# Hybrid decoder layer on one core: repairs at five seams, and transposes ahead of scores in the prompt's attention

## The reference

```python
def decoder_layer(x, nsa_fn, ...):
    xn = rmsnorm(x, g_mix)
    q, kvc, kvs, kvw, gt, mu, mv, mo, mi, mf = split(xn @ w_in)
    o_cmp, o_sel, o_win, ... = nsa_fn(q, kvc, kvs, kvw)
    gates = sigmoid(gt)
    o_nsa = gates[0] * o_cmp + gates[1] * o_sel + gates[2] * o_win
    o_nsa = rmsnorm(o_nsa, g_nsa)
    o_m, ... = mlstm_mixer(mu, mv, mo, mi, mf, ...)   # 4 heads of 128
    h = x + concat([o_m, o_nsa]) @ w_out
    up, f_new = causal_dwconv(rmsnorm(h, g_ffn) @ w_up, f_buf, w_fconv)
    a, g = split(up, 2)
    y = h + (silu(g) * a) @ w_down

def mlstm_mixer(...):
    uc = silu(causal_dwconv(u, conv_buf, w_conv) + b_conv)
    q, k = uc @ w_q, uc @ w_k                          # per head
    hs, C, n, m = mlstm_chunk_scan(q, k, v, ig, fg, C0, n0, m0)
    return (rmsnorm(hs, g_head) + skip * uc) * sigmoid(o)
```

## Time and profile before

| what | us |
|---|---|
| median of 3 runs | 1076.31 |
| lowest, highest | 1075.5, 1076.8 |
| the profiled execution, its own time | 1076.65 |
| its span from first to last instruction | 1074.9 |
| TensorE busy | 1018.1 (95%) |
| VectorE busy | 612.9 (57%) |
| ScalarE busy | 404.1 (38%) |
| GpSimd busy | 152.7 (14%) |

### The profile page before, as it was taken

The page is one execution under the profiler, slowest core; times in us unless marked ns, Lnnn a source line. Parts: engine busy times, 40 slices in busy tenths (PEclk is TensorE's granted clock), DMA queues, the critical chain, the costliest instruction groups (busy, mean ns, idle before and its releaser), DMA issues.

```text
span 1074.9 us, 19288 instructions
## 1 busy us (share of the span) xinstructions
PE 1018.1 (95%) x7776; PEld 917.0 (85%) x7776; DVE 612.9 (57%) x1305; ACT 404.1 (38%) x759; POOL 152.7 (14%) x207
## 2 busy tenths in 40 slices
PE   4999998999999979989899999999999999999996
PEld 4999998999866647665559999999999999999996
DVE  3736753444267656677957336676767677932222
ACT  4223422333143346448764333333333333621212
POOL 3200020330112221016740000000000000000000
PEclk9999999999999989999999999999999999999999
DMA  6561162553511165334012222222222222332322
GB/s 185 186 180 40 56 205 79 209 184 138 240 44 42 42 259 198 122 110 141 2 59 100 78 81 82 81 81 81 81 81 81 81 81 56 91 93 65 96 54 88
DMA packets 82074, 114.26 MB, mean 106 GB/s; under 512 B 10086, under 2 KB 72648, under 8 KB 79263
## 3 DMA queue, kind: packets, MB, share of 16 engines
q1 hardware_dynamic: 75247, 70.60, 21.2%
q0 software_dynamic: 6768, 42.84, 10.8%
HBM read 103.33 MB, written 13.59 MB: 109 GB/s over the span
## 4 chain that ended last, share of the span: by engine, by line
PE 83%; DVE 8%; DMA 3%; ACT 2%; issue 2%; POOL 1%; SPq 0%; DVEq 0%; ACTq 0%
PE banks L1619 14%; PE banks L1617 11%; PE banks L1659 6%; PE banks L1074 5%; PE banks L1129 5%; PE banks L1658 5%; PE banks L1077 4%; PE banks L1078 4%; PE banks L1572 3%; PE banks L1113 2%; PE banks L1571 2%; PE banks L1329 2%; PE banks L1318 2%; PE banks L1690 2%; PE banks L1393 1%
## 5 line engine op out<-in xcount | busy, mean ns | idle before, releaser
L1619 PE MATMUL banks<-xnT_r,RB_r 128*128 128x320 f32 x352 | 109.8, 312 | 0.0
L1619 PE MATMUL banks<-xnT_r,ring_r 128*128 128x320 f32 x352 | 109.4, 311 | 0.0
L1617 PE MATMUL banks<-xnT_r,RB_r 128*128 128x256 f32 x352 | 103.3, 294 | 0.0
L1617 PE MATMUL banks<-xnT_r,ring_r 128*128 128x256 f32 x352 | 98.9, 281 | 0.0
L1619 PE MATMUL banks<-RC_r,RB_r 128*128 128x320 f32 x264 | 82.3, 312 | 0.0
L1129 PE MATMUL banks<-RA,RB 128*128 128x128 f32 (+1 forms) x512 | 71.8, 282 | 2.9 <-DVE RA L1948 1.5
L1617 PE MATMUL banks<-RC_r,RB_r 128*128 128x256 f32 x264 | 74.3, 281 | 0.0
L2345 DVE TENSOR_TENSOR ring_r<-ring,RB_r 128x2048 fp32r<-128x2048 f32 x22 | 49.4, 2289 | 38.1 <-ACT RB_r L886 38.1
L1129 PEld LDWEIGHTS banks<-RA,RB 128*128 128x128 f32 x512 | 65.0, 191 | 4.4 <-ACT RA L668 2.3
L1617 PEld LDWEIGHTS banks<-xnT_r,RB_r 128*128 128x128 f32 x352 | 67.0, 190 | 1.2
L1617 PEld LDWEIGHTS banks<-xnT_r,ring_r 128*128 128x128 f32 x352 | 67.5, 192 | 0.0
(11 more groups left out here) (651 smaller groups left out, 2928.2 us busy)
## 6 DMA issues: line engine op xcount, KB each, us to landing
ring<-in_w_up_dram SPq DMA_DIRECT2D x22, 1024.0 KB
ring<-in_w_down_dram SPq DMA_DIRECT2D x8, 1408.0 KB, 7.0
ring<-in_w_in_dram SPq DMA_DIRECT2D x10, 1024.0 KB, 6.2
RB<-in_state_win_dram SPq DMA_DIRECT2D x8, 512.0 KB
out_win_s_dram<-in_state_win_dram POOLq DMA_DIRECT2D x1, 4032.0 KB
xsp<-RC SPq DMA_DIRECT2D x1, 2304.0 KB, 9.0
xT<-xsp SPq DMA_DIRECT2D x1, 2304.0 KB, 12.9
RA<-in_x_prompt_dram SPq DMA_DIRECT2D x4, 512.0 KB, 5.6
```

The lines of the kernel that those rows point to most:

```text
L1617: t.matmul(ps[4 + par][:, w * UA:(w + 1) * UA], wk[:, w, k, c], x[:, 0:UA], skip_group_check=True, **first)
L1619: last = t.matmul(ps[2 * par + w][:, 0:UB], wk[:, w, k, c], x[:, UA:T], **on)
```

## The change

Five edits at seams, and one in the loop of the prompt's attention.

1. TensorE waits for `c_kcd` behind the transposes of the convolution's rows instead of ahead of them.
2. ScalarE steps `m_proja` behind mkT as well, and TensorE starts pieces 0 and 1 of the product behind that; pieces 2 and 3, into bank 4, wait for mk. Later counts are doubled.
3. VectorE builds `kbd` behind W instead of ahead of `mix_head`.
4. The gating of the last head moves from GpSimd to VectorE, behind the last `mix_head`.
5. In the first pair of the samples, ScalarE evicts the keys q = 2 ahead of `exp_cmp(1)`.
6. In the prompt's attention TensorE's loop has `turn_unit(u - 3)` ahead of `score_unit(u)`.

```diff
@@ -486,7 +486,6 @@
                 out_dma(pool, O["C_p"][0, 0, h], cpo[:, h, :])
             pool.dma_start(O["n_p"][0].rearrange("a h d -> a (h d)"), npo).then_inc(S("m_stored"), 16)
             pool.dma_start(O["n_s"][0].rearrange("b h d -> b (h d)"), nbh).then_inc(S("m_stored"), 16)
-            gated(MH - 1)
             g.memset(Vbd, 0.0).then_inc(S("p_pool"), 1)
 
             pool.wait_ge(S("m_mix"), MH)
@@ -701,7 +700,7 @@
 
                 act.wait_ge(S("m_proj"), h + 1)
                 a.activation(mqT[:, 0:SEQ], ps[0][:, :], ACT.Copy)
-                a.activation(mkT[:, 0:SEQ], ps[2][:, :], ACT.Copy, scale=KSCALE)
+                a.activation(mkT[:, 0:SEQ], ps[2][:, :], ACT.Copy, scale=KSCALE).then_inc(S("m_proja"), 1)
                 a.activation(mk[:, 0:4, :], ps[4][:, :].rearrange("p (i d) -> p i d", i=4), ACT.Copy,
                              scale=KSCALE).then_inc(S("m_proja"), 1)
 
@@ -796,9 +795,11 @@
                     weights_act(p - 1, 1)
                 if p < 4:
                     keys(p, 1)
+                if p == 0:
+                    keys(p, 2)
                 if p < 3:
                     exp_cmp(p + 1)
-                if p < 4:
+                if 0 < p < 4:
                     keys(p, 2)
                 if p:
                     exp_win(p - 1)
@@ -1186,12 +1187,12 @@
             pe.wait_ge(S("c_xa"), 2 + 4 * 8)
             pe.wait_ge(S("c_xd"), 2 + 4 * 8)
             pe.wait_ge(S("c_hid"), 2 + 2 * 8)
-            pe.wait_ge(S("c_kcd"), 2 + 2 * 8)
             pe.wait_ge(S("m_rcol"), 1)
             for k in range(MH):
                 last = t.transpose(ps[5][0:27, k * P:(k + 1) * P], mcg[:, k, :], ident[:])
             last.then_inc(S("m_cols"), 1)
 
+            pe.wait_ge(S("c_kcd"), 2 + 2 * 8)
             pe.wait_ge(S("pool_step"), 6)
             pe.wait_ge(S("m_rows"), 1)
             for kind, row in enumerate((irow, frow, r0)):
@@ -1252,8 +1253,10 @@
                     turn_head(h - 1)
                 turn_states(h, 0)
 
-                pe.wait_ge(S("m_proja"), h + 1)
+                pe.wait_ge(S("m_proja"), 2 * h + 1)
                 for j in range(4):
+                    if j == 2:
+                        pe.wait_ge(S("m_proja"), 2 * h + 2)
                     out = (ps[0][:, :], ps[2][:, 0:384], ps[4][:, 0:256], ps[4][:, 256:384])[j]
                     t.matmul(out, mkT[:, j * P:(j + 1) * P], mqT[:, j * P:SEQ], start=True, stop=True)
                 pe.wait_ge(S("m_projd"), h + 1)
@@ -1296,7 +1299,7 @@
                     last = t.transpose(out, kv[0:rows, i, 256 + 256 * w:384 + 256 * w], ident[0:rows, 0:rows])
             last.then_inc(S("m_cols"), 1)
             turn_head(MH - 1)
-            pe.wait_ge(S("m_proja"), MH + 1)
+            pe.wait_ge(S("m_proja"), 2 * MH + 1)
             pe.wait_ge(S("m_p7d"), 5 * MH)
             def batch_rows(b2):
                 return slice(64 * b2, 64 * b2 + 64)
@@ -1538,10 +1541,10 @@
                 last.then_inc(S("o_turned"), 1)
 
             for u in range(2, NU + 4):
+                if 3 <= u < NU + 3:
+                    turn_unit(u - 3)
                 if u < NU:
                     score_unit(u)
-                if 3 <= u < NU + 3:
-                    turn_unit(u - 3)
                 if u == NU + 3:
                     pe.wait_ge(S("o_sq"), 4)
                     for g in range(GRP - 1):
@@ -2040,6 +2043,10 @@
                                        op0=ALU.mult, op1=ALU.add)
                 v.scalar_tensor_tensor(out=xnT[:, h, SEQ:T], in0=ps[6][:, 258:258 + NSMP], scalar=gh,
                                        in1=ucT[:, h, SEQ:T], op0=ALU.mult, op1=ALU.add).then_inc(S("m_mixd"), 1)
+                if h == MH - 1:
+                    dve.wait_ge(S("m_mixd"), MH)
+                    dve.wait_ge(S("m_mix"), MH - 1)
+                    v.tensor_tensor(xnT[:, h, :], xnT[:, h, :], moT[:, h, :], ALU.mult).then_inc(S("m_mix"), 1)
 
             dve.wait_ge(S("m_proj"), 1)
             decay_sums(0)
@@ -2061,9 +2068,6 @@
                                 rcol[:, 2, 0:4, h:h + 1].to_broadcast([P, 4, P]), ALU.mult)
                 v.tensor_scalar(vw[0:NSMP, 4, :], mv[0:NSMP, 4, h, 0:P], rcol[0:NSMP, 2, 4, h:h + 1], None, ALU.mult)
                 v.tensor_scalar(wlb[0:NSMP, :], bmask, 0.0, rcol[0:NSMP, 2, 4, h:h + 1], ALU.is_equal, ALU.mult)
-                v.scalar_tensor_tensor(out=kbd[0:NSMP, :, :], in0=bmask.unsqueeze(2).to_broadcast([NSMP, NB, P]), scalar=0.0,
-                                       in1=mk[0:NSMP, 4:5, :].to_broadcast([NSMP, NB, P]), op0=ALU.is_equal,
-                                       op1=ALU.mult)
                 if h:
                     if h == 1:
                         dve.wait_ge(S("m_stored"), 4 * 16)
@@ -2078,6 +2082,9 @@
                 v.tensor_tensor(W[:, 896:EW], E[:, 896:EW], ps[4][:, 0:384], ALU.mult)
                 v.tensor_tensor(W[0:NSMP, EW:EW + NSMP], E[0:NSMP, EW:EW + NSMP], ps[4][0:NSMP, 384:384 + NSMP],
                                 ALU.mult).then_inc(S("m_w"), 1)
+                v.scalar_tensor_tensor(out=kbd[0:NSMP, :, :], in0=bmask.unsqueeze(2).to_broadcast([NSMP, NB, P]), scalar=0.0,
+                                       in1=mk[0:NSMP, 4:5, :].to_broadcast([NSMP, NB, P]), op0=ALU.is_equal,
+                                       op1=ALU.mult)
                 dve.wait_ge(S("m_p7"), 5 * h + 2)
                 v.tensor_copy(CT[:, 4:8, 0:P], ps[7][:, :].rearrange("p (b e) -> p b e", b=4)).then_inc(S("m_p7d"), 1)
                 if h < MH - 1:
```

## The result

| | median us | lowest, highest | runs |
|---|---|---|---|
| before | 1076.55 | 1075.5, 1076.98 | 4 |
| after | 1084.3 | 1083.66, 1085.1 | 4 |

The ratio is 1.0073, with a 95% interval from 1.0057 to 1.0089: the change makes the kernel slower by 7.8 us. Forecast were 1082.1, a range from 1070 to 1089, and 0.68 for slower. The profiled execution of after has a span of 1082.7, against 1074.9.

The account below looks back on a forecast made before the run. TensorE was taken to bound the kernel outside the seams, and one unit's way round four engines the prompt's attention. 1076.65 - 6.9 + 10.6 + 2.1 = 1082.4 for the profiled execution, 1082.1 as median; range 1070 to 1089.

Parts of the forecast that it names:

- a ring of dependences: Prompt's attention: scores(u+2) now also need transposes(u-1), hence VectorE's factor, GpSimd's scaling and ScalarE's eviction of unit u-2.
- +10.6: Prompt's attention: cost in us of transposes ahead of scores, last values ending at 569.9 against 559.3.
- the walk: Prompt's attention: all 32 units carried through the engines with the trace's durations, taken as good to about 2 us.
- The clock, +2.1: Prompt's attention: one more fall of TensorE's clock to half rate, some 2.1 us; ends 0 and +8.4.
- The clock's rival: Prompt's attention: the clock falls four times more than before, +8.4, and the walk errs by 2: 1090.8 us; chance 0.08.
- Transposes of unit 1 start at 481.98 as before: Prompt's attention: these wait for GpSimd until 481.92 in either order; scores of unit 4 then start at 483.0, 2.2 later.
- The repairs, -6.9: All edits outside the prompt's attention loop: -0.5 at the first seam, -3.1 in the mLSTM, -3.3 in the first pair.
- Edit 1, -0.5: First seam: four transposes run inside the wait for VectorE, winning 0.53; for the clock nothing taken, ends 0 and -3.
- Edits 2 and 3, -3.1: mLSTM heads 1 to 3: waits of 0.29, 0.50 and 0.83 won, 1.6 in all, and 1.5 of clock in head 2.
- Edit 5, -3.3: Samples' first pair: with the keys first, VectorE's two gaps close, -(2.15 + 1.19), and everything behind follows as before.
- transposes don't only fill gaps: Denies a rival for the prompt's attention: transposes only fill gaps and hold no scores, 1063.9 to 1069.8 us; chance 0.12.
- the ring doesn't bind only at the start: Denies a rival for the prompt's attention: only the loss to unit 8, 3.4 us, stays, giving 1073.2; chance 0.13.

Follow-up runs that it names:

- e2: Kernel before with only the prompt's attention loop reordered, transposes of unit u-3 ahead of scores of unit u: 1089.8 us.
- e3: Changed kernel with older work one unit later in the prompt's attention, transposes of unit u-4 ahead of scores of u, values of u-5 behind: 1066.95 us.
- e12: The same kernel as e3, measured again in a later group of runs: 1065.57 us.
- e4: Changed kernel with GpSimd scaling only the first 128 columns of each head's weights in a unit: 1078.35 us.
- e5: Changed kernel with 62 extra transposes of the identity in TensorE's idle time, ahead of the transposes of units 1, 7, 15, 16, 23 and 24: 1079.6 us.
- e11: Changed kernel with the prompt's loop in its old order, the first seam's wait and GpSimd's last gate also put back as before: 1071.42 us.
- e1: Changed kernel with the prompt's attention loop in its old order, scores ahead of transposes, so the five repairs alone: 1069.19 us.
- e8: Changed kernel with the prompt's loop in its old order, products waiting for both evictions and kbd ahead of W again: 1071.43 us.
- e7: Changed kernel with the prompt's loop in its old order, first pair's keys q = 2 behind pair 1's compressed-score exponentials again: 1072.1 us.
- e6: Changed kernel with transposes ahead of scores only while u < 11 in the prompt's loop, scores first from there on: 1073.26 us.
- e9: Changed kernel with transposes of unit u-4 and values of u-5 in the prompt's loop, but scores ahead of the transposes: 1093.54 us.

## Why the prediction was right, and where it was not

**The sign and the mechanism of edit 6** were right: a ring of dependences through VectorE, GpSimd and ScalarE. Shown: the order alone costs 13.0 (e2), one unit of lag more takes all of it away with the transposes still ahead (e3, e12), and a shorter link moves the waiting to the next (e4). **+10.6** for it measured 11.6 once the clock was held up (e5), and the walk's first units came out within 0.1 us of it, unit 7 and unit 8. Of the unit 4 scores it said 2.2, e5 shows 1.9.

**The clock, +2.1, was the term that was mis-sized.** In after it costs 4.9 (e5), and the trace of before held 1.3 of it already (e11's fall; 85.3 against 84.0), so the term was 3.5 (15.1 less the 11.6 of the order). The step that failed was "TensorE's idle time in this stretch doubles in the walk, so I take two falls in place of one", and it was wrong in both factors. The low time grew from 3.4 us to 20.6, not to twice as much. And a fall costs less than the 2.1 that the step took from the walk's own shortfall: 1.3 for the one in e11, and in after 4.9 for what are six times 3.4 us, 0.8 for each, perhaps since part of each is spent where TensorE would have waited anyway, which no run tests. The clock's rival (four falls more, 1090.8) had the number about right and the price too high. The prediction held against this rival that TensorE idled for 1.00 ahead of 480.79 and stayed at full rate. But its own walk made that wait longer: with the scores moved behind, TensorE idles from 480.79 - 1.00 = 479.79 to 481.98 without a break, 2.2 us, and no wait of TensorE for ScalarE or GpSimd in before was longer than 1.7. In after this wait is 2.93, ahead of the transposes of unit 1, and the clock fell in it.

**"Transposes of unit 1 start at 481.98 as before"** held: 6.06 behind the scores of unit 2, against 6.35. That VectorE would be idle for scores some 10 us more did not: 29.7 us, against 8.2 in the kernel before. The forecast took only the stretch's lengthening as idle time. It lengthened by 15.1, and VectorE's busy time fell by 6 us as well (61.96, against 67.93 in e1): its 32 instructions L2257 take 8.5 us together in after and 15.0 in e1, for the reason in the last section. The row of after:

```profile
DVE banks L2255 <- PE banks L1445: 29.7, 20, 3.4
```

**The repairs, -6.9**, measured -7.6 (e1). That the sums agree so well is partly luck. Between the two traces seam and mLSTM differ by -2.2, the first pair by -3.5, the samples' rest by +1.6 and the prompt's attention by -1.3 through the clock; 2.6 more of e1's lead lie ahead of the seam, where no edit is. By parts:
- Edit 1, -0.5: 0.73 at its place. Behind the seam the clock was low once (3.4 us) in nine of the eleven traces with the edit (e3 and e8 have 6.8; e1, e3 and e4 have another low stretch near 304), and for twice or three times as long in all three without it (before, e2, e11). The prediction took nothing of its bound of -3; e11 suggests one or two us of it, but doesn't settle that.
- Edits 2 and 3, -3.1: 2.2 by e8's median, 2.1 by the stretches of e8 and e3. The waits gave more than their 1.6, and the 1.5 of clock is not to be seen. From the first projection (L1222) to the first numerators, with the clock up in all of them, head 1 takes 10.41 in e8 and 9.90 in after, head 2 10.48 in e8 and 9.90 in e3, head 3 10.41 in e8 and 9.43 in after: 2.1 in all. Head 3 won 0.98, more than the forecast 0.83, though the wait ahead of its numerators fell only from 1.79 to 1.30 and not below the 1.0 that was given as a sign: TensorE comes to this wait 0.49 earlier too, which the sign left out. The 1.48 of clock in head 2 came back elsewhere in most traces: after has it in head 1. That was the step "after the change head 2 looks like head 1, so I take the whole 1.48".
- Edit 4, 0: nothing at its place, as predicted.
- Edit 5, -3.3: 3.4 at its place, by the two gaps. Net it is 2.1 to 2.9, by the ratios and the medians of e7 and e1 (2.6 by the stretches), since the samples' rest gives 1.6 back. That step, "behind the first exponentials of selected scores everything follows as before", held for the order and not for the clock. The edit also took away a stretch of low clock that the prediction doesn't name: around the wait of 3.43, whose scores take 1.97, the clock is low for 6.8 us in all three traces without the edit (from 391.1 in before, 390.6 in e2, 389.0 in e7), and in none of the eleven with it is it low in the first pair. What that is worth by itself isn't told apart.

**The total** of 1082.4 against 1084.4 for the profiled execution is 2.0 short: the prompt's attention took 2.4 more than forecast (1.0 in the walk, 1.4 in the clock) and the samples' rest 1.6; on the other side stand 0.7 more from the repairs' stretches (4.2 and 3.4, against 3.6 and 3.3) and the 1.3 ahead of the seam, which no edit touches. The rivals that would have made it faster fall: transposes don't only fill gaps (the transposes wait 17.2 us), and the ring doesn't bind only at the start (e6).

## What to carry to other kernels

On an engine whose list is in order, an instruction that moves ahead hands its waits to all behind it. Before it is moved, ask what it waits for and whether that could be finished a whole pass earlier: the lag between passes and the place in the pass are one choice, and buffers that are used again (here four, read by transposes(u-4) and written by exponentials(u)) decide which pairs are right. Where a stretch is a ring over several engines, walk it with the trace's durations, unit by unit, for every order that can be written: here such a walk put three new orders within 1 us of the stretch's time with the clock up, the fourth within 5 with the clock low for 17, and found the two whose stretch is the shortest of all (82.0 and 81.6, against 84.0 with the repairs alone). Count what the granted clock does apart from that.

## What the runs showed of the hardware

**The clock falls behind a stretch in which TensorE never idles.** In the samples' rest there is no idle time where it fell; what stands ahead in after is L1421, 64 matmuls of 16 columns each, in 4.37 us; the same 64 stand there in e6, where it did not fall. Three outcomes are seen, and they make that stretch 71.4, 73.0 or 74.6 us: none low (e6, e9), low once (before, e2, e7), low for twice as long (the nine others, after and e1 among them). After, and then e6:

```profile
449.80:452.60 2.80, 2.80 (x53) 2.80 (x52) 1.78 (x5) 0.18 (x2) 0.00 (x0) 1.00 0.07 12
452.80:459.40 6.60, 6.60 (x40) 4.73 (x40) 2.73 (x5) 1.93 (x4) 0.00 (x0) 0.50 0.71 217
```

```profile
450.80:454.50 3.70, 3.70 (x67) 3.67 (x65) 1.80 (x5) 0.20 (x2) 0.00 (x0) 1.00 0.06 9
454.50:461.00 6.50, 6.50 (x70) 4.82 (x70) 5.37 (x10) 2.72 (x6) 0.00 (x0) 1.00 0.78 242
```

All three kernels without edit 5 had it low once, and of the eleven with it nine had it low twice as long: the 3.4 us won ahead of this place went with 1.6 lost at it in those nine. Why was not tried, and two of the eleven had no fall at all.

**Transposes in the waits kept the clock up.** The Trainium skill has it that the full rate doesn't engage for transposes in transpose mode ("TensorE: Matmul & The Clock Gate", Part 4: PE-mode transpose). In e5 the waits were filled with nothing but transposes, and the clock stayed at 1.00 where it had been low for 20.6 us; twenty transposes in one wait took 2.40 us, 0.12 each, and eight at the half clock 1.97, 0.25 each. The trace disagrees, if these are transposes in that mode: it lists them as MATMUL against `ident` and doesn't show the mode.

**A small VectorE instruction waits out GpSimd's.** In after, 128x2 on VectorE (L2257) took 0.17 at 471.93, and 0.90 at 473.45, beside GpSimd's scaling that runs from 472.43 to 474.32:

```profile
471.93 0.17 DVE L2257 TENSOR_SCALAR RA<-RA 128x2 f32<-128x2 f32 x1
...
472.43 1.89 POOL L522 TENSOR_TENSOR RB<-RB,RA 128x1024 f32<-128x1024 f32 x1 [3.24 <-DVE RA L2264]
...
473.45 0.90 DVE L2257 TENSOR_SCALAR RA<-RA 128x2 f32<-128x2 f32 x1
```

It ends at 474.35, as soon as GpSimd does. Of the 32 such instructions 19 start beside a GpSimd instruction in e1, and each of these ends 0.02 to 0.03 behind it; in after it is 11, and all nine that took longer than 0.17 do. Their median is 0.17 in after and 0.43 in e1. The exponentials of the unit wait for it, so this is a link of the ring that no semaphore shows, and the walk held it only as far as it took each duration from its row. By the Trainium skill ("SBUF — State Buffer", SBUF: two separate sides) the port pair that VectorE and GpSimd share is an exclusive lock for the whole instruction, taken by whichever starts first, of a GpSimd instruction and a VectorE one that runs in a 2-port mode or has two SBUF inputs. This row agrees with the lock. L2257 has one SBUF input, and that it ran in a 2-port mode no row shows.
